# Expert weights over a ring of nine 2 MB buffers instead of ten, and the expert loops unrolled by three pairs instead of five

## The chip, the cores and the metric

One core of a Trainium2 chip runs the whole kernel. The metric is the device time of one execution in microseconds; times of a kernel are the median of several runs. A profile is one execution taken by the hardware profiler; its clock starts at the program's first instruction, and "us" below counts from there.

## The reference

One layer of an encoder on 256 tokens of width 1024, float32. The last stage, a mixture of experts, is what the change touches:

```python
def hybrid_layer(x, ...):
    proj = x @ w_in                       # four branches (HGRN2, attention, S5, RG-LRU) from one projection
    ...
    mix = jnp.sum(gates * branch_out, axis=2) @ w_out
    h = layer_norm(DEEPNORM_ALPHA * x + mix, ln1_w, ln1_b)
    ffn = moe_ffn(h, router_w, router_b, moe_w1, moe_b1, moe_w2, moe_b2)
    return layer_norm(DEEPNORM_ALPHA * h + ffn, ln2_w, ln2_b)

# moe_ffn: top 4 of 32 experts per token; per expert
#   clamped_swiglu(xb @ w1[e] + b1[e]) @ w2[e] + b2[e]      w1[e]: 1024 x 2048, w2[e]: 1024 x 1024
```

So each expert has 8 MB of first-layer and 4 MB of second-layer weights, and all 32 experts are read: 384 MB.

## The kernel before

**Stages.** Until about 408 us the projection, the four branches, the merge, the first normalization and the router run; their weights come in 1 MB pieces through a ring of eight slots. Then the experts run one after another. Each takes up to 64 tokens (`CAP`); two experts make a pair, whose tokens are gathered (L1059) and whose results are combined (L1155) together. Expert 0 runs ahead of the loop; then 15 repetitions of "second expert of pair p, first expert of pair p+1"; then expert 31.

**Weights.** An expert's weights are six pieces of 2 MB (`NU = 6`): pieces 0 to 3 are w1 (TensorE reads them on L1109, 16 matmul and 16 weight-load instructions a piece in the profile), pieces 4 and 5 are w2 (L1134, the same number). Piece m of the whole stream (m = 6 * expert + piece, 0 to 191) goes into `buffer[m % NBUF]`. The ten buffers are two in `arena`, six in `ring` (the slots of the first stage), one in `yT` (the branch outputs) and one in `acc_xT`, which holds the transposed input and the merged branches until the expert stage begins.

**Who issues what.** SyncE (SP) issues all weight loads in order. The first ten stand written out, each behind the semaphore that frees its buffer; piece m from 10 on is `reload(m)`, which waits until TensorE has used up piece m - 10 (`expert_chunk_used`), and is then issued. TensorE (PE) waits before each piece for the buffer's `unit_landed`, to which the sixteen parts of a 2 MB transfer add up.

**The loops.** A buffer number must be constant in the code, so PE's and SP's loops repeat only when the sequence of buffers does: `ROUND` pairs are unrolled per round, 15 pairs in 15 / `ROUND` rounds, and `2 * ROUND * NU` must be a multiple of `NBUF`. PE's round stands at L1177 to L1189, SP's at L382. VectorE and ScalarE loop over single pairs and don't know the buffers. In the built program PE's round is 2,696 instructions long, SP's 242.

**The end.** After the last round come expert 31, the combination of the last pair on top of the sum, the last normalization and the output (L1813 to L1826, L397).

Of the kernel before, what the change touches and what calls it, by code (L numbers as in the profile page):

```python
# [54 lines left out]
NSLOT = 12  # L55
NU = 6
NW1 = 4
NBUF = 10
ROUND = 5
UNIT = 2 * SLOT  # L60


# [35 lines left out]
def encoder_layer(nc, A, out, dbg=None):  # L98
    with ExitStack() as ctx:
        def sb(name, shape, dt=F32):  # L100
            return ctx.enter_context(nc.sbuf_tensor(name, shape, dt))

        def sem(name):
            return ctx.enter_context(nc.semaphore(name))
# [21 lines left out]
        acc_xT = sb("acc_xT", [P, 2 * KD, SEQ])  # L126
# [125 lines left out]
        landed = [sem(f"landed{i}") for i in range(R1)]  # L252
        unit_landed = [sem(f"unit_landed{i}") for i in range(NBUF)]
        names = """chunk_used const_ready iota_ready iota_read vec_in s5_in lru_in pos_in ones_ready s5_small s5_mag s5_theta s5_trig0 exp_ready prep_psum prep_evac f_ready trig_ready bu_psum bu_free x_ready x_used
# [19 lines left out]
        def used_up(*c):  # L274
            return STREAM.index(c) + 1

        def slot(s, *shape):
            n = int(np.prod(shape))
            v = ring[:, s * SLOT:s * SLOT + n]
            names = "abcd"[:len(shape)]  # L280
            return v.rearrange(f"p ({' '.join(names)}) -> p {' '.join(names)}", **dict(zip(names[1:], shape[1:])))
# [4 lines left out]
        def chunk_source(c):  # L286
            if c[0] in COL:
                w = 192 if c[0] == "ckv" else CW
                return (KD, w), A["w_in"][PROJ.index(c), :, 0:KD * w].rearrange("p (k n) -> p k n", k=KD)
            if c[0] == "wglu":  # L290
                return (4, 512), A["s5_w_glu"].rearrange("(k p) n -> p k n", p=P)
            if c[0] == "wq":
                return (2, 768), A["mla_wq_b"].rearrange("(k p) n -> p k n", p=P)
            if c[0] == "wkv":
                return (1, 1024), A["mla_wkv_b"].rearrange("(k p) n -> p k n", p=P)
            if c[0] == "wb":
                return (4, 512), A["w_branch"][c[1], c[2]].rearrange("p (k n) -> p k n", k=4)
            return (2, D), A["w_out"][256 * c[1]:256 * c[1] + 256, :].rearrange("(k p) n -> p k n", p=P)
# [9 lines left out]
        def expert_source(e, c):  # L308

            if c < NW1:  # L310
                return w1[e, 256 * c:256 * c + 256, :].rearrange("(p k) n -> p (k n)", k=2)
            return w2[e, 512 * (c - NW1):512 * (c - NW1) + 512, :].rearrange("(p k) n -> p (k n)", k=4)

        def unit_of(i):
            return ring[:, i * UNIT:(i + 1) * UNIT]

        buffer = [arena_unit[0], arena_unit[1], unit_of(0), unit_of(1), unit_of(4), unit_of(5), yT[:, :, :, :].rearrange("p a b c -> p (a b c)"),
                  unit_of(2), unit_of(3), acc_xT.rearrange("p a b -> p (a b)")]
        assert len(buffer) == NBUF and (NPAIR - 1) % ROUND == 0 and 2 * ROUND * NU % NBUF == 0
        ln2_w = buffer[4][:, 0:D]  # L320
        TURNS = 2 * ROUND * NU // NBUF

        def unit_buffer(n, c):
            return (n * NU + c) % NBUF

        def unit_count(n, c, q=0):

            return 16 * ((n * NU + c) // NBUF + 1) + q * (16 * TURNS)

        def item_buffer(c):  # L330
            return (6 + c) % NBUF

# [4 lines left out]
        @block.sync  # L337
        def _(sp):

            def load(e, c, i):  # L340
                sp.dma_start(buffer[i], expert_source(e, c)).then_inc(unit_landed[i], 16)

            x_rows = A["xT"].rearrange("p (k t) -> p k t", k=KD)
            shape, src = chunk_source(STREAM[0])
            first = slot(slot_of[STREAM[0]], *shape)
            for i in range(pieces):
                ks = slice(KD // pieces * i, KD // pieces * (i + 1))
                sp.dma_start(xT[:, ks, :], x_rows[:, ks, :]).then_inc(first_in[i], 16)
                sp.dma_start(first[:, ks, :], src[:, ks, :]).then_inc(first_in[i], 16)
            for i, c in enumerate(STREAM):  # L350
                if i == 0:
                    continue
                if c == ("wo", 0):
                    sp.wait_ge(S["cross_ready"], 1)
                    load(0, 0, 0)
                if i >= R1:
                    sp.wait_ge(S["chunk_used"], i - R1 + 1)
                shape, src = chunk_source(c)
                sp.dma_start(slot(slot_of[c], *shape), src).then_inc(landed[i % R1], 16)

            sp.wait_ge(S["yA_ready"], 2)
            load(0, 1, 1)
            sp.wait_ge(S["chunk_used"], used_up("wb", 1, 1))
            load(0, 2, 2)
            sp.wait_ge(S["chunk_used"], used_up("wb", 0, 1))
            load(0, 3, 3)
            sp.wait_ge(S["acc_ready"], 4)
            load(0, 4, 4)
            load(0, 5, 5)
            load(1, 0, 6)  # L370
            sp.wait_ge(S["chunk_used"], used_up("wo", 1))
            load(1, 1, 7)
            sp.wait_ge(S["chunk_used"], used_up("wo", 3))
            load(1, 2, 8)
            load(1, 3, 9)

            def reload(m, q=0):

                sp.wait_ge(S["expert_chunk_used"], q * (2 * ROUND * NU) + (m - NBUF + 1))
                load(q * (2 * ROUND) + m // NU, m % NU, m % NBUF)  # L380

            with sp.Fori(0, (NPAIR - 1) // ROUND) as q:  # L382
                for m in range(NBUF, NBUF + 2 * ROUND * NU):
                    reload(m, q)
            for m in range(NBUF + 2 * (NPAIR - 1) * NU, NE * NU):
                reload(m)

            sp.wait_ge(S["items_ready"], 1)
            n_items = sp.value_load(item_e[0:1, NITEM:NITEM + 1], min_val=0, max_val=NITEM)
            with sp.If(n_items > 0):  # L390
                with sp.Fori(0, n_items) as j:
                    e = sp.value_load(item_e[0:1, bass.ds(j, 1)], min_val=0, max_val=NE - 1)
                    for c in range(NU):
                        sp.wait_ge(S["expert_chunk_used"], j * NU + NE * NU)
                        load(e, c, item_buffer(c))
            sp.wait_ge(S["out_ready"], 1)
            sp.dma_start(out[0][0:P, :], y_acc[:, 0, :]).then_inc(S["out_sent"], 16)  # L397
            for dh in range(2):
                sp.wait_ge(S["out_ready"], 2 + dh)
                sp.dma_start(out[0][P:2 * P, 512 * dh:512 * dh + 512], y_acc[:, 1, 512 * dh:512 * dh + 512]).then_inc(S["out_sent"], 16)  # L400
            sp.wait_ge(S["out_sent"], 48)
# [1489 lines left out]
```

## Time and profile before

| what | value |
| --- | --- |
| median of 3 runs (lowest, highest) | 1342.42 us (1342.34, 1343.73) |
| the profiled execution's own time | 1343.0 us |
| its span, first to last instruction | 1341.1 us |
| PE matmuls busy | 1261.6 us, 94% |
| VectorE, ScalarE busy | 452.3 us (34%), 212.2 us (16%) |
| mean granted TensorE clock | 0.99 |
| moved by DMA | 458.05 MB, 342 GB/s over the span |
| chain that ended last | PE 58%, DMA 36% |

Shares over the whole span mix two stages: ahead of 408 us DMA is mostly idle, from about 450 us on it is busy all the time. The 32 experts take the last 933 us.

### The profile page before, as it was taken

To read this page: it belongs to the slowest core of one execution; us is meant where nothing else is said; L and a number is where in the kernel's file an instruction comes from. 1 tells how busy PE (TensorE), PEld (TensorE's weight loads), DVE (VectorE), ACT (ScalarE), POOL (GpSimd) and SP (SyncE) were. 2 spreads that over 40 slices of the span, in tenths; PEclk is the share of its full clock that TensorE was granted. 3 is DMA by queue.
4 is the path that set the end of the run, shared out by engine and by line. 5 is a ranking of instruction groups with operands and counts; after the bars stand their busy time and mean duration, and the time that the engine had idled before them with its cause. 6 is when DMAs were issued, how large, how long until landed. Compare 5 with 4: busy or idle time off the path is not lost.

```text
span 1341.1 us, 15697 instructions
## 1 busy us (share of the span) xinstructions
PE 1261.6 (94%) x6210; PEld 664.5 (50%) x6210; DVE 452.3 (34%) x915; ACT 212.2 (16%) x419; POOL 4.0 (0%) x20
## 2 busy tenths in 40 slices
PE   9999999999999999999999888999989899989895
PEld 8888877898854434434434333433324333333331
DVE  5589766356433521221321212222121212212123
ACT  1522214222012101101101010110101011010101
POOL 0000000000000000000000000000000000000000
PEclk9999999999998999999999999999999999999998
DMA  9433334315788999999999999999999999999991
GB/s 375 168 126 126 110 110 158 126 64 190 253 350 328 409 430 427 427 429 428 428 426 426 429 429 428 426 427 429 428 427 427 426 428 429 427 428 428 427 428 81
DMA packets 39515, 458.05 MB, mean 342 GB/s; under 512 B 5620, under 2 KB 6004, under 8 KB 10008
## 3 DMA queue, kind: packets, MB, share of 16 engines
q1 hardware_dynamic: 36304, 453.00, 81.2%
q10 hardware_dynamic: 3144, 4.04, 0.9%
q8 instruction: 56, 0.92, 0.3%
q14 instruction: 11, 0.09, 0.0%
HBM read 455.98 MB, written 1.05 MB: 341 GB/s over the span
## 4 chain that ended last, share of the span: by engine, by line
PE 58%; DMA 36%; DVE 4%; ACT 1%; issue 1%; SPq 0%; DVEq 0%; ACTq 0%
DMA ring<-in_moe_w 22%; PE banks L745 13%; PE banks L1109 12%; PE banks L1134 11%; DMA arena<-in_moe_w 6%; DMA acc_xT<-in_moe_w 6%; PE banks L1155 4%; PE banks L759 4%; PE banks L1059 2%; PE banks L1023 2%; PE banks L890 1%; PE banks L732 1%; PE banks L997 1%; PE banks L991 1%; PE banks L1118 1%; PE banks L809 1%
## 5 line engine op out<-in xcount | busy, mean ns | idle before, releaser
L1109 PE MATMUL banks<-ring,arena 128*64 128x512 f32 x1216 | 273.5, 594 | 31.7 <-DMA ring<-in_moe_w 31.4
L745 PE MATMUL banks<-acc_xT,ring 128*128 128x256 f32 x896 | 198.5, 381 | 0.0
L1109 PEld LDWEIGHTS banks<-ring,arena 128*64 128x64 f32 x1216 | 94.7, 137 | 208.0 <-issue 203.6
L745 PEld LDWEIGHTS banks<-acc_xT,ring 128*128 128x128 f32 x896 | 168.8, 190 | 28.2 <-issue 6.0
L1714 DVE TENSOR_SCALAR arena<-banks 128x512 f32<-128x512 f32 x32 | 22.1, 691 | 460.3 <-PE banks L1109 460.3
L1134 PE MATMUL banks<-ring,arena 128*64 128x512 f32 x608 | 135.8, 596 | 0.0
L1109 PE MATMUL banks<-arena 128*64 128x512 f32 x416 | 93.5, 595 | 10.9 <-DMA arena<-in_moe_w 10.7
L1726 DVE COPY arena<-banks 64x512 f32<-64x512 f32 x32 | 22.2, 694 | 239.3 <-PE banks L1134 239.3
L669 ACT ACTIVATE arena<-arena 128x512 f32<-128x512 f32 x32 | 20.2, 630 | 505.4 <-DVE arena L1714 505.3
L1134 PEld LDWEIGHTS banks<-ring,arena 128*64 128x64 f32 x608 | 42.0, 137 | 92.2 <-issue 77.6
L1109 PEld LDWEIGHTS banks<-arena 128*64 128x64 f32 x416 | 30.3, 137 | 71.9 <-issue 63.6
L1059 PE MATMUL banks<-arena 128*128 128x128 f32 x512 | 63.4, 285 | 2.1 <-DVE arena L1692 2.1
L1059 PEld LDWEIGHTS banks<-arena 128*128 128x128 f32 x512 | 61.9, 201 | 2.8 <-DVE arena L1692 2.3
L1109 PE MATMUL banks<-yT,arena 128*64 128x512 f32 x208 | 50.0, 612 | 11.1 <-issue 6.1
L1155 PE MATMUL banks<-arena 128*128 128x512 f32 x128 | 59.2, 605 | 1.0 <-DVE arena L1726 1.0
L759 PE MATMUL banks<-yT,ring 128*128 128x256 f32 x256 | 56.2, 379 | 0.1
L759 PEld LDWEIGHTS banks<-yT,ring 128*128 128x128 f32 x256 | 48.3, 190 | 7.3 <-issue 1.0
L1134 PE MATMUL banks<-arena 128*64 128x512 f32 x224 | 51.3, 611 | 0.7 <-ACT arena L673 0.7
L1109 PE MATMUL banks<-acc_xT,arena 128*64 128x512 f32 x208 | 47.4, 595 | 3.4 <-DMA acc_xT<-in_moe_w 3.3
L677 ACT ACTIVATE arena<-banks 64x512 f32<-64x512 f32 x32 | 18.9, 589 | 198.9 <-PE banks L1134 198.9
L658 ACT ACTIVATE arena<-banks,ln_cols 128x128 f32<-128x128 f32 x128 | 46.4, 474 | 6.6 <-PE banks L1059 6.6
L1155 PEld LDWEIGHTS banks<-arena 128*128 128x128 f32 x128 | 23.0, 189 | 37.0 <-issue 37.0
(369 smaller groups left out, 1040.5 us busy)
## 6 DMA issues: line engine op xcount, KB each, us to landing
ring<-in_moe_w SPq DMA_DIRECT2D x114, 2048.0 KB, 42.4
arena<-in_moe_w SPq DMA_DIRECT2D x40, 2048.0 KB, 42.5
yT<-in_moe_w SPq DMA_DIRECT2D x19, 2048.0 KB, 40.9
acc_xT<-in_moe_w SPq DMA_DIRECT2D x19, 2048.0 KB, 42.7
ring<-in_w_in SPq DMA_DIRECT2D x30, 1024.0 KB, 4.9
ring<-in_w_branch SPq DMA_DIRECT2D x8, 1024.0 KB, 4.8
ring<-in_w_out SPq DMA_DIRECT2D x4, 1024.0 KB, 6.4
acc_xT<-in_xT SPq DMA_DIRECT2D x2, 512.0 KB, 5.5
```

The costliest lines, as they stand in the source:

```text
L658: ins = nc.scalar.activation(xg[:, k, :], bank[2 + k // 4][:, (k % 4) * P:(k % 4 + 1) * P], ACT.Identity, scale=ln1_cols[:, 2 * KD + k:2 * ...
L669: nc.scalar.activation(g3, g1, ACT.Sigmoid, scale=SWA).then_inc(S["sig_ready"], 1)
L677: nc.scalar.activation(y_pair[64 * u:64 * u + 64, 0:512], bank[4][0:64, :], ACT.Copy).then_inc(S["ypair_act"], 1)
L745: last = mm(b[:, j * SEQ:(j + 1) * SEQ], w[:, k, j * P:j * P + P], xT[:, k, :], start=k == 0, stop=k == KD - 1)
L759: last = mm(bank[3 + u % 2][:, i * SEQ:(i + 1) * SEQ], w[:, k, c * P:(c + 1) * P], yT[:, br, k, :], start=k == 0, stop=k == 3)
L1023: mm(bank[i][64 * ct:64 * ct + 64, :], esel[r:r + NE, :], b1_all[r:r + NE, :], start=True, stop=False, tile_position=(r, 64 * ct))
L1059: last = mm(bank[2 + k // 4][:, (k % 4) * P:(k % 4) * P + cols], h_tok[:, half, k * P:k * P + P], sel[:, half, 0:cols], start=half == 0, s ...
L1109: last = mm(bank[i][64 * ct:64 * ct + 64, :], xg[:, 2 * c + kk, col:col + CAP], w[:, kk, i * FF + ct * 512:i * FF + ct * 512 + 512], start ...
L1134: last = mm(bank[4][64 * dh:64 * dh + 64, :], actT[:, j, 64 * fh:64 * fh + 64], w[:, j, 512 * dh:512 * dh + 512], start=(fh, j) == (0, 0), ...
L1155: mm(bank[COMB_BANK[i]][:, :], wselT[0:rows_, half, :], y_pair[0:rows_, 512 * dh:512 * dh + 512], start=not on_sum, stop=True).then_inc(S[ ...
L1714: V.tensor_scalar(g1, bank[0][:, :], LIMIT, None, ALU.min).then_inc(S["gmin_ready"], 1)
L1726: V.tensor_copy(y_pair[64 * u:64 * u + 64, 512:1024], bank[4][64:128, :]).then_inc(S["ypair_vec"], 1)
```

## The change

The buffer in `acc_xT` is taken out of the ring of weight buffers, so pieces go into `buffer[m % 9]`, the written-out loads end with piece 8, and `reload(m)` waits until piece m - 9 is used up. Since the sequence of nine buffers repeats after 36 pieces, the round is three pairs, and the loops of PE and SP go round five times instead of three. The loads, the matmuls and their order are the same. The functions that use `NBUF` and `ROUND` (`reload`, `unit_buffer`, `unit_count`, the two loops) are not edited.

```diff
-NBUF = 10
-ROUND = 5
+NBUF = 9
+ROUND = 3
@@
         buffer = [arena_unit[0], arena_unit[1], unit_of(0), unit_of(1), unit_of(4), unit_of(5), yT[:, :, :, :].rearrange("p a b c -> p (a b c)"),
-                  unit_of(2), unit_of(3), acc_xT.rearrange("p a b -> p (a b)")]
+                  unit_of(2), unit_of(3)]
@@
             sp.wait_ge(S["chunk_used"], used_up("wo", 3))
             load(1, 2, 8)
-            load(1, 3, 9)
```

On SP, this is where the written-out loads end and the loop begins, after the branches' merge; `ISA [waits expert_chunk_used]` is the wait of one `reload`. Before:

```order
L341 DMA ring<-in_moe_w 128x4096 [waits chunk_used] x2
L341 DMA acc_xT<-in_moe_w 128x4096
L382 UNCONDITIONAL_BRANCH
L382 ISA
L341 ISA [waits expert_chunk_used]
L341 DMA arena<-in_moe_w 128x4096
```

After:

```order
L341 DMA ring<-in_moe_w 128x4096 [waits chunk_used] x2
L381 UNCONDITIONAL_BRANCH
L381 ISA
L341 ISA [waits expert_chunk_used]
L341 DMA arena<-in_moe_w 128x4096
```

The load into `acc_xT`, piece 9, is gone from its place ahead of the loop; the first load behind a wait for a used piece was piece 10 and is now piece 9, in the same `arena` buffer.

On PE, this is the end of a round: the second-layer matmuls of its last expert, the branch back, and behind it expert 31. Before:

```order
L1155 MATMUL banks<-arena 128x512 x4
L1116 REGISTER_ALU
L1118 MATMUL banks<-ident,arena 128x128 x4
L1019 REGISTER_ALU
L1023 MATMUL banks<-arena 64x512 x4
L1134 MATMUL banks<-ring,arena 64x512 x16
L1177 REGISTER_ALU
L1177 COMPARE_AND_BRANCH
L1109 MATMUL banks<-yT,arena 64x512 x8
```

After:

```order
L1154 MATMUL banks<-arena 128x512 x4
L1115 REGISTER_ALU
L1117 MATMUL banks<-ident,arena 128x128 x4
L1018 REGISTER_ALU
L1022 MATMUL banks<-arena 64x512 x4
L1133 MATMUL banks<-ring,arena 64x512 x16
L1176 REGISTER_ALU
L1176 COMPARE_AND_BRANCH
L1108 MATMUL banks<-yT,arena 64x512 x8
```

The same rows stand there, but between them and the round's first matmul lie 1,620 instructions instead of 2,696, and the branch is taken four times instead of twice. (All lines of the code behind the removed one are lower by one.)

## Rows read from the trace of the kernel before

**Rows 1.** The page, part 2: DMA busy tenths and GB/s in 40 slices

```profile
DMA  9433334315788999999999999999999999999991
GB/s 375 168 126 126 110 110 158 126 64 190 253 350 328 409 430 427 427 429 428 428 426 426 429 429 428 426 427 429 428 427 427 426 428 429 427 428 428 427 428 81
```

**Rows 2.** Waits, 690 to 1284 us: us in total, times, longest

```profile
PE banks L1109 <- DMA ring<-in_moe_w: 31.0, 29, 1.3
PE banks L1109 <- DMA arena<-in_moe_w: 10.7, 10, 1.3
...
PE banks L1109 <- DMA yT<-in_moe_w: 4.9, 4, 1.2
PE banks L1109 <- DMA acc_xT<-in_moe_w: 3.3, 4, 1.3
```

**Rows 3.** Timeline of PE, 511 to 566 us: start, us, instruction, count

```profile
512.57 7.09 PE L1134 MATMUL banks<-ring,arena 128*64 128x512 f32 x32
...
564.55 1.94 PE L1134 MATMUL banks<-ring,arena 128*64 128x512 f32 x8
```

**Rows 4.** Timeline of PE, 1155 to 1181 us; idle time before, and its releaser, in brackets

```profile
1159.25 3.65 PE L1109 MATMUL banks<-acc_xT,arena 128*64 128x512 f32 x16 [1.25 <-DMA acc_xT<-in_moe_w]
...
1175.45 3.65 PE L1109 MATMUL banks<-ring,arena 128*64 128x512 f32 x16 [0.45 <-DMA ring<-in_moe_w]
1180.35 1.08 PE L1109 MATMUL banks<-ring,arena 128*64 128x512 f32 x4 [1.24 <-DMA ring<-in_moe_w]
```

**Rows 5.** Timeline of PE, 1272 us to the end

```profile
1278.22 3.65 PE L1109 MATMUL banks<-ring,arena 128*64 128x512 f32 x16 [1.23 <-DMA ring<-in_moe_w]
...
1286.89 7.09 PE L1134 MATMUL banks<-ring,arena 128*64 128x512 f32 x32
...
1318.09 8.74 PE L1134 MATMUL banks<-arena 128*64 128x512 f32 x32 [0.69 <-ACT arena L673]
```

**Rows 6.** Timeline of SP, 390 to 425 us: its DMA issues

```profile
390.68 5.94 SPq L341 DMA_DIRECT2D ring<-in_moe_w  x2
396.66 0.43 SPq L341 DMA_DIRECT2D acc_xT<-in_moe_w  x1
412.27 3.73 SPq L341 DMA_DIRECT2D arena<-in_moe_w  x2
```

**Rows 7.** Landing times of the two loads issued at 396.3 and 396.7 us

```profile
DMA to landing us min/median/max: 7.6/9.9/12.1
```

**Rows 8.** Landing times of the loads issued from 516 to 560 us

```profile
DMA to landing us min/median/max: 16.6/21.9/27.4
```

**Rows 9.** Landing times of the loads issued from 781 to 1272 us

```profile
DMA to landing us min/median/max: 40.6/45.0/46.5
```

**Rows 10.** PE's branch, line L1177: duration ns min/median/max, first and last start

```profile
L1177 PEldq COMPARE_BRANCH  x3: 83/6032/6358, 697.7 to 1289.6; - x3
```

**Rows 11.** Timeline of PE around its first taken branch, 690 to 715 us

```profile
694.96 7.09 PE L1134 MATMUL banks<-ring,arena 128*64 128x512 f32 x32
704.05 3.64 PE L1109 MATMUL banks<-yT,arena 128*64 128x512 f32 x15 [2.01 <-issue]
709.30 0.59 PE L1109 MATMUL banks<-yT,arena 128*64 128x512 f32 x1 [1.60 <-issue]
```

**Rows 12.** DMA queues, 701 to 996 us (PE's second round): packets, MB, share

```profile
q8 instruction: 13, 0.21, 0.3%
```

**Rows 13.** DMA queues, 644 to 786 us: packets, MB, share

```profile
q8 instruction: 8, 0.13, 0.4%
```

**Rows 14.** DMA queues, 577 to 1272 us: all that moved anything

```profile
q1 hardware_dynamic: 20365, 296.59, 100.4%
q8 instruction: 30, 0.49, 0.3%
```

**Rows 15.** SP's branch, line L382, 670 to 685 us: duration ns min/median/max

```profile
L382 SPq COMPARE_BRANCH  x1: 50/50/50, 676.2 to 676.2; - x1
```

**Rows 16.** Windows, PE's second round: PE busy and count, PEld busy and count, ...

```profile
704.00:997.30 293.30, 266.67 (x1290) 106.39 (x1290) 56.38 (x116) 32.88 (x75) 0.00 (x0) 1.00 1.01 428
```

## The prediction

> **What bounds the kernel now.** I read the page's forty slices first [rows 1]: from slice 15 on DMA is busy nine tenths and moves 426 to 430 GB/s whatever the engines do. A flat line like this is a limit, not a demand. Then the waits: between 690 and 1284 us PE waits for landings of weights 47 times, 49.9 us in all, never more than 1.3 us at once [rows 2], so every piece is taken as soon as it has landed. The pitch of landings stands in the starts of two neighbouring pieces that both waited, 1180.35 - 1175.45 = 4.90 us for 2 MB [rows 4]; I use 4.89, the mean of the undisturbed ones. An expert costs DMA 6 x 4.89 = 29.3 us. PE, where it doesn't wait, needs 26.0 us: 51.98 us for the two experts between 512.57 and 564.55 [rows 3]. So PE, which is behind a full ring at first, catches up by 3.3 us an expert and from about 690 us on hangs on DMA.
>
> The last wait for a landing is that of piece 183 at 1278.22; from there to the end PE, VectorE and ScalarE run 62.9 us of their own work, and the last pieces have landed before they are wanted [rows 5]. If all landings come later by some time, so does that wait, and the tail moves with it unchanged. The end is therefore (when the stream of loads starts) + (what it carries) + (what delays it).
>
> **The missing buffer.** Before, SP issues pieces 7, 8 and 9 at 390.7, 396.3 and 396.7, all ahead of the first expert, and piece 10 at 412.27, when PE has used up piece 0 [rows 6]. Pieces 8 and 9 land at 396.3 + 7.6 = 403.9 and 396.7 + 12.1 = 408.8 [rows 7]. After, piece 9 is the first to wait for a used piece: it goes at 412.27, piece 10 when piece 10 - 9 = 1 is used, and so on. Each issue time of before now belongs to the piece one lower: the queue is filled at the same moments with the same sizes, but one piece is missing from it, and DMA idles 4.89 us longer ahead of 412 us. From then on piece n lands when piece n + 1 did, and the last wait comes one pitch later: **+4.89 us**. It could be hidden only if DMA had a hole later; the flat rate [rows 1] and the 47 waits [rows 2] leave none.
>
> Does a shallower queue slow the rate? A load lands 40.6 to 46.5 us after its issue in the bound stretch [rows 9], that is 8 to 9 pitches, so 8 to 9 loads are outstanding, and 7 to 8 after. In the stretch 516 to 560 us only 3 to 5 are outstanding (16.6 to 27.4 us [rows 8]), and the slices of that stretch (the 16th and 17th) run at the same 427 GB/s. So the rate stays: 0.
>
> **The two added branches back.** PE's branch takes 83 ns where it falls through and 6.0 and 6.4 us where it is taken [rows 10]. After the first taken one PE idles 2.01 us, then 1.60 us more [rows 11]; with slower matmuls around them that expert takes 30.5 us instead of 26.0. What the branch waits for is its code: q8 carries instruction packets of 16 KB, 13 in the second round [rows 12], which has 1290 matmuls, as many weight loads [rows 16] and 116 others. 2,696 instructions by 256 a packet are 10.5 packets; so at the jump the target isn't there any more, the packets are fetched anew from the target's on, and one more is fetched ahead of the round's end and thrown away. SP's branch takes 50 ns [rows 15]: its 242 instructions stay loaded, and no other instruction packet than PE's comes in all this time [rows 14].
>
> After, the branch is taken behind pieces 41, 77, 113 and 149, at about 597, 766, 944 and 1121 us. The stall itself is covered: PE has 3.3 us to gain on DMA per expert, the last jump is five experts before the last wait (16 us to gain for 4.5), and 7 loads outstanding (34 us) feed DMA meanwhile. The first jump delays the freeing of buffers by 4.5 us while 4 to 5 loads are outstanding. Cost 0; without that cover it would be 4.5 us a jump.
>
> **The packets themselves** are not free. The pitch is broken in few places: pieces 159 and 162 both waited, and lie 16.20 us apart instead of 3 x 4.89 = 14.68 [rows 4], 1.5 us too much. From piece 40 on I find four such steps, at the landings of pieces 55, 84, 127 and 162, each just behind an instruction packet (644, 787, 997, 1171 us), and with exactly eight packets from one to the next [rows 13]. The parts of a load's landing show why: every packet delays one of the sixteen by 1.5 us, going round eight of them, and the piece counts as landed with the last. So eight packets cost 1.5 us of the end, 0.19 us each.
>
> How many packets will there be? It depends on whether a round of 1,620 instructions, 6.3 packets, stays loaded as SP's 242 do, or is thrown out as the 2,696 are. No row of before decides it; the bounds are these. *Stays*: no packet between about 600 and 1284 us, all four steps vanish, -4 x 1.5 = -6.1 us. *Thrown out*: nine packets in each of five rounds, 42 instead of 36 from 464 to 1290 us, and counting every eighth from the first jump gives five steps instead of four, +1.5 us. I take the second: 1,620 lies nearer to 2,696, and there is a placement. Setting each packet between the waits of PE's sequencer puts the round's first instruction about 199 of 256 into its packet; so it spans eight packets, the last by 26 instructions, and with the one ahead nine must be held.
>
> The Trainium skill ("Runtime: NRT & Kernel Launch", section "Instruction fetch mechanics") says that instructions come in blocks of 256, which the trace agrees with (16 KB packets), and that a taken branch whose target is outside the current window of two pages waits for a fetch. By that rule the packets are thrown out here, and the sum is +6.4 us; SP's 50 ns speak against a window that small. The same section gives TensorE's instruction memory as 2,048 instructions, which would be room for 1,620 and a sum of -1.2 us, but not for nine blocks. So the two statements of the page lead to different times, and only the second round's packets will tell.
>
> **Sum.** +4.89 (missing buffer) + 0 (rate, jumps) + 1.5 (one more step) = +6.4 us. The profiled execution took 1343.0 us, 0.6 above the median of 1342.42; as differences carry over, I predict **1348.8 us**. This case's own range is 1346.8 to 1350.4: the fifth step may not fall on the part that is last (-1.5), or one more may (+1.5), and runs spread by 1.4 us.
>
> **Rivals.**
> - *The round stays loaded* (0.12): +4.89 - 6.1 = -1.2 us, 1341.2 us, no change that can be told. For it: SP's loop stays, and the round shrinks by two fifths. Against: the placement above. It decides from eight held packets on down: if PE holds nine, this is the case.
> - *The load is hidden anyway* (0.04): 1342.4, or 1343.9 with one more step. It needs holes in the stream; rows 1 and 2 show none.
> - *The queue runs dry at the jumps* (0.05): four jumps by 4.5 us on top of the sum, up to 1366.8 us. It needs fewer than two loads outstanding; rows 8 and 9 leave at least three.
> - *Faster*, the other side (0.03): the round stays loaded and fewer interrupted parts let the loads run faster still. More than the four steps' 6.1 us isn't there to win from packets, so beyond 1341.2 it needs 1.5 us more: the landing step at the stream's start (near 470 us) would have to go as well. 1339.7 us.
>
> **How the numbers follow.** A measurement of this kernel tells 0.2%, 2.7 us, from no change (runs spread by 1.4 us). The forecast case has 0.76. Slower takes it and the dry queue: 0.82 with a little of the second rival; same takes the loaded round and most of the hidden load: 0.15; faster 0.03. The range 1344.6 to 1350.8 holds the forecast case with its bounds and the low case of +2.3 us in which a step or two are saved; the loaded round, 1341.2, is left out with the tail above: 2 in 10.
>
> **What would show it.** Right: `ring`, `arena` and `yT` carry all 192 loads, the load issued at 412.27 is piece 9, the landing time in the bound stretch falls from 45.0 to about 40 us; PE's branch comes five times, four at 6 us; q8 carries about 63 packets instead of 56, nine a round; waits for DMA begin one or two experts earlier; DMA stays at 427 GB/s to the end, and the last wait, 1278.22 now, comes at about 1284.6. Wrong: if the branch takes 50 to 100 ns each time and q8 carries about 27 packets, the loaded round has won, and the last wait comes at 1277.0. If the rate between 600 and 1284 us drops below 425 GB/s, the shallower queue cost more than I say. If the last wait moved by 6.4 us and the end did not, my reading of the tail is wrong.

## The result, and the profile of the changed kernel

The changed kernel takes 1348.51 us, median of 7 runs (1345.42 to 1349.4); the kernel before, beside it, 1342.34 us, also of 7 (1340.45 to 1343.73). The ratio is 1.0041, with a 95% interval of 1.0032 to 1.0051: slower by 6.2 us, where 1348.8 was forecast. The profiled execution took 1348.63 us, with a span of 1346.8.

The page's forty slices of the changed kernel, which answer to [rows 1]:

```profile
DMA  9433334315787999999999999999999999999991
GB/s 376 165 126 125 109 110 157 125 68 191 271 331 280 425 431 427 427 426 428 428 427 428 427 428 427 428 427 426 426 427 428 427 428 427 428 428 428 428 417 72
```

The slice that shows the missing load best is the thirteenth, from 404 to 438 us: 280 GB/s instead of 328. Its nearest neighbours differ by 16 to 19 GB/s in either direction, and from the fifteenth to the thirty-eighth the two rows agree within 3 GB/s. SP's timeline, against [rows 6], has no load at 396.66 any more, and its first wait for a used piece ends with piece 9, 2.4 us sooner than before's with piece 10, because this execution was that much earlier:

```profile
390.37 5.94 SPq L341 DMA_DIRECT2D ring<-in_moe_w  x2
409.91 3.72 SPq L341 DMA_DIRECT2D arena<-in_moe_w  x2
```

PE's waits from 690 to 1284 us, against [rows 2], are about as many (45) and as long (46.3 us for landings); new in size is what PE loses at the branches, put down as issue (12.0 us, before 6.1):

```profile
PE banks L1108 <- DMA ring<-in_moe_w: 31.6, 30, 1.3
PE banks L1108 <- issue: 12.0, 6, 2.3
PE banks L1108 <- DMA yT<-in_moe_w: 8.6, 7, 1.3
PE banks L1108 <- DMA arena<-in_moe_w: 6.1, 8, 1.3
```

Three more views: the landing times of the loads issued from 781 to 1272 us (against [rows 9]), PE's branch (against [rows 10]), and the instruction packets from 594 to 762 us, one round (against [rows 12]):

```profile
DMA to landing us min/median/max: 34.1/39.3/41.7
```

```profile
L1176 PEldq COMPARE_BRANCH  x5: 83/6097/6348, 590.7 to 1293.8; - x5
```

```profile
q8 instruction: 9, 0.15, 0.4%
```

A load lands 5.7 us sooner after its issue than before, of which 4.9 are the one load that no longer stands ahead of it, and no sooner in absolute time. The branch is taken four times at 6 us, and every round, short as it is, has its nine packets fetched anew.

Last PE's timeline at the first expert and at the end, against [rows 5]:

```profile
402.28 3.81 PE L1058 MATMUL banks<-arena 128*128 128x128 f32 x32 [0.31 <-DVE arena L1630]
406.02 4.51 PE L1108 MATMUL banks<-arena 128*64 128x512 f32 x20
...
1282.42 3.65 PE L1108 MATMUL banks<-ring,arena 128*64 128x512 f32 x16 [1.24 <-DMA ring<-in_moe_w]
...
1322.28 6.67 PE L1133 MATMUL banks<-arena 128*64 128x512 f32 x16 [0.69 <-ACT arena L672]
1328.78 3.60 PE L1133 MATMUL banks<-ring,arena 128*64 128x512 f32 x16
```

In the kernel before, the first expert's first matmul is this:

```profile
408.40 1.94 PE L1109 MATMUL banks<-arena 128*64 128x512 f32 x8
```

From the first expert's first matmul to the last piece that PE waited for (183) it is 1282.42 - 406.02 = 876.40 us; before it was 1278.22 - 408.40 = 869.82. This is the measure for all that follows, as it leaves out what differs by chance ahead of it and behind. Here it is +6.58 us. The span's difference of 5.7 us is then -2.38 (the first expert came sooner) + 6.58 + 1.50 (from the last wait to the end 64.4 us instead of 62.9). The first and the last term are for the most part TensorE's clock, in these rows of the windows, the changed kernel's first and then before's:

```profile
402.00:408.00 6.00, 5.72 (x42) 4.42 (x44) 2.68 (x4) 3.36 (x9) 0.00 (x0) 1.00 0.12 49
1322.00:1332.00 10.00, 9.72 (x32) 2.88 (x32) 0.00 (x0) 0.22 (x1) 0.00 (x0) 0.68 0.01 2
```

```profile
402.00:408.00 6.00, 6.00 (x32) 5.49 (x33) 3.15 (x6) 1.40 (x4) 0.00 (x0) 0.61 0.96 410
1322.00:1332.00 10.00, 9.00 (x36) 3.09 (x32) 3.40 (x7) 2.07 (x3) 0.00 (x0) 1.00 0.01 2
```

The seventh number is the granted clock, 1.00 and 0.68 against 0.61 and 1.00, so in each execution one of the two stretches ran partly at 1.2 GHz instead of 2.4. Both kinds of kernel show both: the end took 64.2 us in a run with ten buffers and 62.7 in one with nine, below. The 32 matmuls just ahead of the first expert (L1058) took 3.81 us here and 5.66 before, 1.85 of the 2.38 us.

### The profile page after: what moved, and what is told of

Read it like the earlier page. It is cut to its first block, busy times and chain, and to the rows that moved or that the text cites. A ratio compares the mean times of both kernels' runs of the same rounds, so it can differ in the third digit from the quotient of the medians.

```text
span 1346.8 us, 15713 instructions
## 1 busy us (share of the span) xinstructions
PE 1262.4 (94%) x6210; PEld 666.9 (50%) x6210; DVE 452.1 (34%) x915; ACT 212.2 (16%) x419; POOL 4.0 (0%) x20
## 4 chain that ended last, share of the span: by engine, by line
PE 60%; DMA 33%; DVE 4%; issue 2%; ACT 1%; SPq 0%; DVEq 0%; ACTq 0%
DMA ring<-in_moe_w 18%; PE banks L1108 16%; PE banks L744 13%; PE banks L1133 10%; DMA yT<-in_moe_w 9%; DMA arena<-in_moe_w 5%; PE banks L758 4%; PE banks L1154 3%; PE banks L1058 2%; PE banks L1022 1%; PE banks L889 1%; PE banks L731 1%; PE banks L996 1%; PE banks L990 1%; PE banks L1117 1%
## 5 line engine op out<-in xcount | busy, mean ns | idle before, releaser
L1108 PE MATMUL banks<-ring,arena 128*64 128x512 f32 x1184 | 267.4, 597 | 31.7 <-DMA ring<-in_moe_w 31.6
L1108 PEld LDWEIGHTS banks<-ring,arena 128*64 128x64 f32 x1184 | 96.7, 137 | 205.5 <-issue 196.7
L1133 PE MATMUL banks<-ring,arena 128*64 128x512 f32 x848 | 189.4, 597 | 0.0
L1108 PE MATMUL banks<-arena 128*64 128x512 f32 x528 | 119.5, 595 | 7.0 <-DMA arena<-in_moe_w 6.9
L1133 PEld LDWEIGHTS banks<-ring,arena 128*64 128x64 f32 x848 | 59.3, 138 | 128.0 <-issue 111.7
L1108 PE MATMUL banks<-yT,arena 128*64 128x512 f32 x336 | 80.4, 606 | 22.7 <-issue 14.0
L1108 PEld LDWEIGHTS banks<-arena 128*64 128x64 f32 x528 | 41.1, 137 | 81.4 <-issue 68.3
L1058 PE MATMUL banks<-arena 128*128 128x128 f32 x512 | 60.0, 275 | 2.4 <-DVE arena L1691 2.1
L1058 PEld LDWEIGHTS banks<-arena 128*128 128x128 f32 x512 | 58.4, 192 | 3.0 <-DVE arena L1691 2.3
L1108 PEld LDWEIGHTS banks<-yT,arena 128*64 128x64 f32 x336 | 25.1, 139 | 68.1 <-issue 68.1
L1133 PE MATMUL banks<-arena 128*64 128x512 f32 x176 | 43.2, 636 | 0.7 <-ACT arena L672 0.7
L1154 PEld LDWEIGHTS banks<-arena 128*128 128x128 f32 x128 | 23.0, 189 | 37.1 <-issue 37.1
```

Of the source, the lines that this page charges most:

```text
L1058: last = mm(bank[2 + k // 4][:, (k % 4) * P:(k % 4) * P + cols], h_tok[:, half, k * P:k * P + P], sel[:, half, 0:cols], start=half == 0, s ...
L1108: last = mm(bank[i][64 * ct:64 * ct + 64, :], xg[:, 2 * c + kk, col:col + CAP], w[:, kk, i * FF + ct * 512:i * FF + ct * 512 + 512], start ...
L1133: last = mm(bank[4][64 * dh:64 * dh + 64, :], actT[:, j, 64 * fh:64 * fh + 64], w[:, j, 512 * dh:512 * dh + 512], start=(fh, j) == (0, 0), ...
L1154: mm(bank[COMB_BANK[i]][:, :], wselT[0:rows_, half, :], y_pair[0:rows_, 512 * dh:512 * dh + 512], start=not on_sum, stop=True).then_inc(S[ ...
```

## The experiments

The theory on trial, A: one piece missing from the stream costs 4.9 us, and the rest is instruction packets, 1.5 us for eight of them, fetched because the round and what is fetched ahead need nine places. Against it stand B (branches are all the cost, the missing load is hidden) and C (a shallower queue costs by itself). The column of packets counts q8 between 450 and 1290 us. A ratio compares with runs of the kernel before taken beside: their median was 1342.61 us for lag_one, lag_late, straight_nine and shift_round, 1342.26 for lag_later, straight_ten and the two that begin with ten_to, and 1342.21 for dead_code; beside the two single runs it took 1343.3. The fourth column is from one profiled execution each, and scatters by up to about 2 us.

| kernel | buffers | median us (runs) | first expert to piece 183, us | packets |
|---|---|---|---|---|
| before | 10 | 1342.34 (7) | 869.82 | 36 |
| changed | 9 | 1348.51 (7) | 876.40 | 41 |
| lag_one | 10, used as 9 | 1347.37 (5) | 874.71 | 36 |
| lag_late | 10, as 9 from piece 20 | 1346.65 (5) | 871.98 | 35 |
| lag_later | 10, as 9 from piece 40 | 1342.61 (11) | 869.98 | 36 |
| straight_nine | 9 | 1347.37 (5) | 873.72 | 30 |
| straight_ten | 10 | 1342.88 (11) | 869.09 | 30 |
| shift_round | 9 | 1341.73 (11) | 869.58 | 6 |
| shift_215 | 9 | 1342.87 (1) | 871.12 | 14 |
| shift_240 | 9 | 1348.18 (1) | 876.31 | 41 |
| ten_to_19 | 9, a tenth once | 1343.27 (11) | 867.74 | 12 |
| ten_to_45 | 9, a tenth up to piece 45 | 1339.75 (12) | 865.01 | 12 |
| dead_code | 9 | 1342.79 (11) | 867.70 | 6 |

**The missing load alone.** Ten buffers and rounds of five pairs, but the queue filled as with nine:

```
+            sp.wait_ge(S["expert_chunk_used"], 1)
             load(1, 3, 9)
...
-                sp.wait_ge(S["expert_chunk_used"], q * (2 * ROUND * NU) + (m - NBUF + 1))
+                sp.wait_ge(S["expert_chunk_used"], q * (2 * ROUND * NU) + (m - NBUF + 2))
```

> The kernel before with its ten buffers and its rounds of five pairs, but with the queue of loads filled as the changed kernel fills it: piece 9 waits for the first used piece, and every reload for one used piece more. Theory A (a piece missing from the stream of loads costs one pitch, 4.89 us, once; the rest of the change's 6.2 us is instruction packets): +4.9 us over before, 1347.2 us, 1346.3 to 1348.2; 56 packets on q8 as before, steps of 1.4 us at four places in the round's part, the last wait for DMA 4.9 us later than before's when both are counted from the first expert. Theory B (the cost is in the two added branches and their refetched packets, and the missing buffer is hidden): no change, 1342.4 us. Theory C (a shallower queue slows every load): more than 6 us, and fewer than 426 GB/s between 690 and 1280 us.

Measured: ratio 1.0037 (1.0023 to 1.005), 1347.37 beside 1342.61 us, +4.8. The first expert's first matmul and the last wait, with the 56 packets unchanged:

```profile
407.38 1.94 PE L1110 MATMUL banks<-arena 128*64 128x512 f32 x8
...
1282.09 3.65 PE L1110 MATMUL banks<-ring,arena 128*64 128x512 f32 x16 [1.25 <-DMA ring<-in_moe_w]
```

1282.09 - 407.38 = 874.71, which is 4.89 more than before: one pitch. That it fits to the hundredth is chance, given the scatter; the interval of the ratio is 3.1 to 6.7 us. It holds the pitch and rules out no change, so B is out. C asked for more than 6 us, which the median doesn't show but the interval reaches; the next two runs are about C. One detail was missed: the steps of 1.4 us at four places are here spread over many smaller ones (one of 5.8 us where 4.9 is the pitch, the others under 5.7), since the parts of a load no longer lie as they did; the sum is the same.

**Shallower only later.** The same reload line with `(m >= 2 * NBUF)` added instead of the constant, and in the second run `(m >= 4 * NBUF)`:

```
-                sp.wait_ge(S["expert_chunk_used"], q * (2 * ROUND * NU) + (m - NBUF + 1))
+                sp.wait_ge(S["expert_chunk_used"], q * (2 * ROUND * NU) + (m - NBUF + 1 + (m >= 2 * NBUF)))
```

> The kernel before with its first ten loads and the ten reloads behind them issued as before, and the other fifty reloads of each round one used piece later. In most of the run the queue is then as deep as the changed kernel's, but nothing is missing from it at the start. Theory A (only the start of the stream counts, since the queue is never empty later): no change, within 0.7 us of before's 1342.4; landing time in the bound stretch about 40 us instead of 45. Theory C (depth itself costs): a large part of the 6 us, 1346 to 1349 us.

Measured: ratio 1.0034 (1.0021 to 1.0048), 1346.65 us, +4.0: the expectation of no change fell, and the time lies in the range that C gave. SP's timeline shows a hole that I had overlooked, here and in the kernel before:

```profile
451.13 0.33 SPq L341 DMA_DIRECT2D acc_xT<-in_moe_w  x1
467.53 3.77 SPq L341 DMA_DIRECT2D arena<-in_moe_w  x2
```

```profile
464.42 3.77 SPq L341 DMA_DIRECT2D arena<-in_moe_w  x2
```

PE frees nothing for 13 us between two experts here, and piece 20 now goes out at 467.53, in the moment in which piece 19 lands (467.51); before it went 3.3 us ahead of that. So the start of the stream isn't over at 412 us. The landings of single pieces show three places where the queue is nearly empty. In the kernel before, piece 10 lands 11.3 us behind piece 9, piece 14 lands 8.0 us behind piece 13 (near 434 us), and piece 20 lands 6.5 us behind piece 19 (near 465 us), where the pitch is 4.89. In the changed kernel piece 9 lands 13.8 us behind piece 8 and piece 13 lands 9.9 us behind piece 12, and near 465 us there is no gap. The profiled execution lost 2.2 us between its first expert and piece 183, and was the fastest of its five; what makes the other 1.8 us of the median isn't settled. The second run moves the limit to where three and more loads are outstanding:

> As the run that held reloads back by one used piece from piece 20 on, but from piece 40 on. Worked out from before's rows by a ledger (a load lands 7.6 us after its issue or 4.89 us after the load ahead of it, whichever is later): before's piece 20 is issued only 1.9 us ahead of the end of the queue, so that run lost 3.4 us there and this one should lose nothing, as 3 or more loads are outstanding from piece 30 on. Theory A (a withheld piece costs only where it lets the queue run empty): within 0.7 us of before, 1342.6 us. Theory C (a shallower queue in the bound stretch costs by itself): again 1346 to 1347 us.

Measured: 1342.61 beside 1342.26 us, ratio 1.0006 (0.9997 to 1.0014), 869.98 us against 869.82; loads issued from 781 us on land after a median of 40.2 us. That is nearly the queue of the changed kernel (39.3 us) over the whole bound stretch, free of charge. C, which asked for 1346 us or more, is out.

**No branch.** The loop written out for all fifteen pairs, with nine buffers and with ten:

```
-ROUND = 3
+ROUND = 15
```

> The changed kernel's nine buffers with the loop written out for all fifteen pairs: no taken branch, no packet fetched twice; about 31 packets over the stretch in which the changed kernel has 42 and before 36. Theory A: missing buffer +4.9, and 31 packets make three or four steps of 1.4 us (before four, changed five): +3.4 to +4.9 us over before, 1345.8 to 1347.3 us. Theory B (branches and packets are all the cost): 1342.4 us or less. If the stalls at the branches cost time by themselves, as the case in which the queue runs dry says, it falls below 1345.8.

> The kernel before with its ten buffers and the loop written out for all fifteen pairs: no taken branch, 31 instruction packets instead of 36 behind piece 20. Theory A: the same as before less at most one step of 1.4 us, 1341.2 to 1342.6 us, and 4.9 us below the nine buffers written out (1347.4). If a taken branch costs time beyond its packets, two of them vanish: below 1341 us.

Measured: 1347.37 us with nine (ratio 1.0037, 1.0024 to 1.0051), 1342.88 with ten (1.0001, 0.9992 to 1.001), 4.5 apart, or 4.1 when each is taken against the before beside it, and 0.1 and 0.3 us above the expected ranges; from the first expert to piece 183 it is +3.90 and -0.73 against before, 4.63 apart. The missing buffer costs the same where no branch is taken at all. The medians lie 0.9 and 1.3 us above what these differences say (1346.5 and 1341.5 us, from the before beside each); the likely reason, a later start, comes last.

**Shifting the round.** The loop isn't touched. A hundred instructions among PE's first projections, waits for what has long come (two waits in the code make one instruction in the trace), move it:

```
                         for k in range(KD):
                             last = mm(b[:, j * SEQ:(j + 1) * SEQ], w[:, k, j * P:j * P + P], xT[:, k, :], start=k == 0, stop=k == KD - 1)
+                            if padded[0] < 100:
+                                padded[0] += 1
+                                for _ in range(2):
+                                    pe.wait_ge(S["ones_ready"], 1)
```

> The changed kernel with 100 waits for a semaphore that has long been up among PE's first projections. They do nothing but move the round by 100 instructions: by my placement it then begins 42 into its packet of 256 instead of 199, and spans seven packets instead of eight. Theory A (PE holds eight packets, the one fetched ahead among them, so nine threw the round out): the taken branch falls from 6 us to under 0.1 us, the packets between 600 and 1290 us vanish (q8 about 27 instead of 62), and with them four or five steps of 1.4 us: 1341.3 to 1342.9 us, beside 1348.5 of the changed kernel. Theory D (a taken branch back over more than a packet or two is always fetched anew, whatever the round spans): 62 packets, 6 us a branch, 1348.5 us. If the waits themselves cost time, it shows ahead of 100 us, at most 2 us.

Measured: 1341.73 us, ratio to before 0.9997 (0.9988 to 1.0006), and 6.8 us under the changed kernel. The branch, what moved on the queues from 600 to 1290 us, and the first expert's first matmul with the last wait:

```profile
L1181 PEldq COMPARE_BRANCH  x5: 76/208/236, 591.0 to 1287.3; - x5
```

```profile
q1 hardware_dynamic: 20303, 295.69, 100.7%
```

```profile
406.31 3.22 PE L1113 MATMUL banks<-arena 128*64 128x512 f32 x14
...
1275.89 3.65 PE L1113 MATMUL banks<-ring,arena 128*64 128x512 f32 x16 [1.24 <-DMA ring<-in_moe_w]
```

The second view has one row: no packet of any engine's instructions comes in 690 us. The taken branch costs 0.2 us where under 0.1 was expected. Theory D is out. A hundred instructions that do nothing made the kernel faster, by where they put the ones behind them. Two more kernels, run once each, seek the edge, with 215 and with 240 in place of 100:

> The changed kernel with 215 harmless waits among PE's first projections instead of the 100 of the shifted round. By my placement the round now begins 158 into its packet of 256 and ends 14 short of the end of its seventh packet. Theory A (what counts is how many packets the round spans, seven stay and eight don't): about 26 instruction packets, branches under 0.1 us, about 1341.7 us. Theory E (the shifted round stayed only because its start lay near the front of a packet, or for another reason of its own): 62 packets and 6 us a branch, 1348.5 us.

> The same with 240 waits, 25 more: the round begins 183 into its packet and its last ten or so instructions fall into an eighth packet. Theory A: thrown out again, about 62 packets, four branches of about 6 us, about 1348.5 us, by 25 instructions alone. Theory E or a placement that is off by more than 14 instructions: as the run with 215.

PE's branch and q8 from 600 to 1290 us, first with 215, then with 240:

```profile
L1181 PEldq COMPARE_BRANCH  x5: 76/229/6087, 590.9 to 1288.9; - x5
```

```profile
q8 instruction: 7, 0.11, 0.1%
```

```profile
L1181 PEldq COMPARE_BRANCH  x5: 83/6213/6358, 592.0 to 1295.0; - x5
```

```profile
q8 instruction: 34, 0.56, 0.3%
```

With 240 it is thrown out at every jump again, 1348.18 us. With 215, 14 instructions short of the edge by my placement, it is thrown out at the first jump only (6.1 us) and stays from the second on, 1342.87 us. At the first jump a ninth packet was fetched (at 591.7 us, 0.8 us after the branch began); in the second round eight came, and no ninth, and the round stayed. So 25 instructions decide between 14 and 41 packets, and theory E is out; why the first round at that edge fetched one more than the second stays open.

**A version that beats both.** The round as shifted, and a tenth buffer only while the stream starts. The first three pairs are written out ahead of the loop, so that the buffer numbers inside the loop stay constant, with 30 harmless waits to place it:

```
+        def piece_buffer(m):
+            return m % (NBUF + 1) if m < 40 else (m - 40) % NBUF
...
+                sp.wait_ge(S["expert_chunk_used"], q * (2 * ROUND * NU) + (m - NBUF + (m >= 46)))
...
+            for r in range(ROUND):
+                pair(r)
+            with pe.Fori(0, (NPAIR - 1) // ROUND - 1) as q:
+                for r in range(ROUND, 2 * ROUND):
+                    pair(r, q)
```

ten_to_19 uses it for piece 9 alone, with `return m if m <= NBUF else (m - 1) % NBUF` and `(m > 2 * NBUF)`.

> The changed kernel with its first three pairs written out ahead of the loop, the round placed so that it spans seven packets, and a tenth buffer used once, for piece 9: pieces up to 18 wait for the tenth piece back, as in the kernel before, and all from 19 on for the ninth, as in the changed one. By the ledger the queue has run empty once more when piece 19 is issued (3.0 us after the landing of piece 18), so the 4.9 us won at piece 9 are lost again there: no better than the round shifted alone, 1341.0 to 1342.4 us. If it were enough to fill the hole ahead of piece 9: 1336.8 us.

> The same, but the tenth buffer takes pieces 9, 19, 29 and 39, and only from piece 46 on do loads wait for the ninth piece back, when four or more loads are outstanding by the ledger. Nothing is then missing from the stream, and the round stays loaded, so no packets between about 690 and 1290 us. Theory A: 4.9 us under the shifted round's 1341.7, 1336.8 us, 1335.8 to 1338.2; DMA's landings up to piece 45 as before's. Theory C (nine buffers cost in the bound stretch): 1340 us or more.

Measured: 1343.27 us (ratio to before 1.0006, 0.9997 to 1.0015) and 1339.75 us (0.998, 0.9971 to 0.9988). ten_to_45 is 2.5 us faster than the kernel before and 8.8 faster than the changed one. Both versions lie above their expected ranges, by 0.9 and 1.6 us. The branch of ten_to_45, its first expert's first matmul and its last wait:

```profile
L1204 PEldq COMPARE_BRANCH  x4: 76/210/236, 756.0 to 1284.6; - x4
```

```profile
408.15 1.08 PE L1122 MATMUL banks<-arena 128*64 128x512 f32 x4
...
1273.16 3.65 PE L1122 MATMUL banks<-ring,arena 128*64 128x512 f32 x16 [1.25 <-DMA ring<-in_moe_w]
```

From the first expert on it gains 4.81 us on before, and 4.57 on shift_round, nearly the pitch that was expected. Between the two versions lie 2.73 us, where the ledger had said 4.9: the ledger lands loads too early where the queue is nearly empty but another load is still under way (before's pieces 14 and 20 land 9.0 and 9.8 us after their issue, and more than a pitch behind the one ahead). It so takes the stream to be further ahead than it is, and prices the emptying of the queue too high: it has piece 18 of ten_to_19 landed 3.0 us ahead of piece 19's issue, and in the trace it is 0.4 us (461.89 and 462.24). The same holds for lag_late, 3.4 us by the ledger and 2.2 in the trace. The median of ten_to_45 is still 2.9 us above the 1336.8 expected. Its profiled execution gives back 1.8 us on shift_round's ahead of the first expert, and 0.9 behind the last wait. The first of these shows at the very start of the trace. PE's first projection in it, and in shift_round:

```profile
7.85 1.99 PE L791 MATMUL banks<-acc_xT,ring 128*128 128x256 f32 x8 [1.74 <-DMA ring<-in_w_in]
```

```profile
6.19 1.99 PE L782 MATMUL banks<-acc_xT,ring 128*128 128x256 f32 x8 [0.74 <-DMA ring<-in_w_in]
```

The four kernels with pairs written out all begin it at 7.4 to 7.9 us, the others at 6.2 to 6.4, and they come to the merge's last matmuls, just ahead of the first expert, at 403.0 to 403.4 us instead of 401.3 to 402.0. The last run asks whether length alone does that:

```
             with pe.If(n_items > 0):
...
+                for _ in range(3200):
+                    pe.wait_ge(S["ones_ready"], 1)
```

> The shifted round (100 harmless waits ahead, nine buffers, round of seven packets) with 1,600 more instructions in a part of PE's program that is jumped over. The kernels with written-out pairs began their first projection 1.0 to 1.4 us later than the others (7.4 to 7.9 us instead of 6.2 to 6.4) and were 1.5 to 2.1 us late from there to the first expert. Theory F (a longer program delays the start by itself): the first projection at 7.3 us or later, and 1.5 to 2 us over the shifted round: 1343.3 to 1343.8 us. Rival (it came from what is executed, or from another part of those edits): first projection at 6.2 to 6.4 us and 1341.7 us. Either way about 26 instruction packets and branches under 0.3 us.

```profile
7.65 3.68 PE L782 MATMUL banks<-acc_xT,ring 128*128 128x256 f32 x8 [2.34 <-DMA ring<-in_w_in]
```

Measured: the first projection at 7.65 us, and VectorE's instructions 1.5 us behind shift_round's from there on, by code that is never run. The median is 1342.79 us, 1.1 above shift_round's 1341.73 and 0.5 below the least that was expected, but the runs spread from 1339.81 to 1344.4, so the delay is shown and its price in the end is not. What in a longer program holds back the first input wasn't tried.

## Why the prediction was right

- **Bound by DMA, and the tail moves with the last wait.** Right. The measure from first expert to last wait went up by 6.58 us, and the time by 6.2. The tail moved with it but for the clock's 1.5 us, which the profiled execution had gained ahead of the first expert. That 1282.42 was seen where 1284.6 was forecast is the 2.4 us by which the first expert came sooner, less 0.2.
- **Missing buffer, +4.89.** Shown on its own: +4.89 in the trace of lag_one, +4.8 in its time, and 4.63 between the two kernels without branches. The reason as given is in part wrong, and the number owes something to luck. The prediction said that no later hole could hide the missing piece, but before's stream has two, near 434 and near 465 us. "The queue is filled at the same moments" fails near 434: piece 13 is issued 27.5 us after the first expert's first matmul, where before's piece 14 was issued at 25.9, and the gap there grew by 1.9 us; the gap near 465, 1.6 us over the pitch, closed. The two nearly cancel, so that piece 20 lands 70.96 us after the first expert's first matmul instead of 65.83, 5.1 us later. The clock has a part in this. In the six kernels with a piece missing from the start and a granted clock of 0.76 between 424 and 438 us, the changed one among them, piece 20 lands at 70.3 to 71.2 us; in dead_code, with 0.88, it lands at 68.8, where the missing piece has cost 3.0 us. With the queue filled as before up to piece 20 it lands at 65.5 to 66.5, at 0.88 (the kernel before) as at 0.76. One execution with 0.88 is little, and no run tried this on its own.
- **Depth, 0.** Right: lag_later has nearly the landing time of the changed kernel (40.2 and 39.3 us; about 40 was forecast) and the time of the one before.
- **Two more taken branches, 0.** Right as far as seen: four jumps of 6 us, PE idle for 1.8 to 2.3 us at a stretch, up to 4.3 a jump, and DMA at 427 GB/s throughout. Waits for DMA begin in earnest at 708.6 us instead of 740.1, one expert earlier.
- **Packets, +1.5.** Right in kind and number: nine a round, 62 in all where about 63 were forecast (56 before), and five steps (at the landings of pieces 46, 79, 114, 144 and 174, 6.3 us instead of 4.9), each just behind a packet, with eight packets from one to the next. From piece 20 to piece 183 the changed kernel loses 6.58 - 5.13 = 1.45 us more. Over the kernels with nine buffers, 41 packets against the 6 of shift_round cost 876.40 - 869.58 = 6.8 us, 0.19 each, as the 1.5 us by eight had it. Single executions scatter by some 2 us about that line, so the price of a packet is rough: dead_code, also with 6 packets, lies 1.9 below shift_round, 1.4 of it from before piece 20, in the stretch with the other clock.
- **The round is thrown out because it needs nine packets.** This was the choice on which the sign hung. That the placement decides is now shown: spans of seven stay, but for the first jump at the very edge, spans of eight are thrown out, and the rival priced at 1341.2 us is the kernel that 100 instructions of shift make, 1341.73 us. That the limit is eight packets held is the reading that fits all of them, shift_215 too, where the jump behind nine packets missed and the one behind eight didn't; the spans are worked out from the times of packets, and no run varied the round's length. Two reasons of the prediction fall. That 1,620 lies nearer to 2,696 says nothing, since shift_round's 1,620 stay. And SP's 50 ns don't speak against a window of two packets, since its 242 instructions touch two packets of 256 at most. By the same placement the round would have stayed, and the kernel been no slower, had it begun some 27 instructions earlier in its packet: the working found where it lay, but where it lay was accident. The Trainium skill ("Runtime: NRT & Kernel Launch", section "Instruction fetch mechanics") gives TensorE's instruction memory as 2,048 instructions in blocks of 256, which is eight blocks; the placements here agree with that number. It also says that a taken branch waits for a fetch when its target isn't in the current window of two pages, and here the traces differ: in shift_round PE jumps back over 1,620 instructions in 0.2 us and fetches nothing.

## What to carry to other kernels

- Where DMA is the bound, count a removed buffer as a piece missing from the stream at its start, about one pitch, and look for every place at which the queue runs nearly empty. The one piece of depth that was tested beyond that is worth nothing, so a spare buffer need only be spare while the queue is short.
- PE's loop is cheap if all of it stays loaded, and what decides it here is how many packets the loop touches, not how many instructions it has. Read the packets of one round on q8: none, or all of them. If it is all and the round is near the limit, shift the loop before rewriting it.
- Fetched instructions share the DMA engines with the data: about 0.19 us a packet here, although the branches' own stalls were covered.

## What the runs showed of the hardware that was not expected

- PE kept a round of 1,620 instructions over seven packets through four jumps, 0.2 us each and no packet in 690 us, and lost it when 140 more instructions stood ahead of it.
- An instruction packet of 16 KB, 0.8% of a load, costs its DMA part 1.5 us. With eight parts hit in turn the loads' last parts move only with every eighth packet, so the time goes in steps; after another start of the stream the same sum comes in many small ones.
- 1,600 instructions that are never executed moved the first projection from 6.19 to 7.65 us.
- The same kernel's clock falls to 1.2 GHz for a few us at the first expert or at the end in some executions, and this alone moves single times by 1.4 to 1.9 us. A third such stretch lies between 424 and 438 us (0.88 in four of the thirteen traces, 0.76 in nine). Effects of this size show in medians only.
